# A hybrid decoder trunk on eight cores: the program rewritten with even token groups, the norm factor applied to results, and one mLSTM chain between the dense units

## What is computed

```python
# x: (8, 2048, 2048); 16 meta tokens are put ahead of each sequence
for l in range(2):
    proj = rmsnorm(h, norm_mix_w[l]) @ w_in[l]              # 2048 -> 6152
    q, k, v, og, ig, fg, u, gb, gc = jnp.split(proj, split_points, axis=-1)
    hm = mlstm_group(q, k, v, ig + b_i, fg + b_f)           # 4 heads, qk 128, v 256, chunkwise
    hm = jax.nn.sigmoid(og) * rmsnorm_per_head(hm, mlstm_norm_w[l])
    hc = gb * causal_conv3(gc * u, conv_w[l])
    h = h + jnp.concatenate([hm, hc], axis=-1) @ w_out[l]
    hf = rmsnorm(h, norm_ffn_w[l])
    h = h + (silu(hf @ w_gate[l]) * (hf @ w_up[l])) @ w_down[l]   # width 5632
return rmsnorm(h, norm_final_w)[:, 16:]
```

## Time and profile before

| | us |
|---|---|
| median of 3 runs (lowest to highest) | 6702.95 (6699.74 to 7196.77) |
| span of the profiled execution, slowest core | 6697.5 |
| TensorE matmul busy in it | 5962.8 (89%) |
| VectorE busy | 1665.9 (25%) |
| ScalarE busy | 878.2 (13%) |
| GpSimd busy | 460.8 (7%) |

### The profile page before, as it was taken

One profiled execution on the slowest core, in us unless ns is written; L12 is line 12 of the kernel. 1 busy time (PEld: TensorE's weight loads), 2 busy tenths in 40 slices (PEclk: granted clock), 3 DMA queues, 4 the chain that ended last, 5 costly groups with the idle time before them and its releaser, 6 DMA issues.

```text
span 6697.5 us, 83763 instructions; the slowest of 8 cores (6676.9 to 6697.5 us)
## 1 busy us (share of the span) xinstructions
PE 5962.8 (89%) x33182; PEld 2840.1 (42%) x33822; DVE 1665.9 (25%) x3868; ACT 878.2 (13%) x1988; POOL 460.8 (7%) x416
## 2 busy tenths in 40 slices
PE   5885999999788599999977968999998987999997
PEld 3442444444344244444443433444443433344444
DVE  2333211111333321111133432111113532211113
ACT  2212100000121210000022121000002221100002
POOL 0110000000011000000000100000000100000000
PEclk7997999999899799999988988999998998999998
DMA  4662556655365245655553654665564763655653
GB/s 83 56 61 32 60 70 73 76 70 72 49 60 57 35 59 71 73 76 70 71 125 53 67 57 51 69 79 77 71 76 54 73 62 46 69 71 74 82 77 81
DMA packets 814720, 450.64 MB, mean 67 GB/s; under 512 B 277488, under 2 KB 810096, under 8 KB 810224
## 3 DMA queue, kind: packets, MB, share of 16 engines
q0 software_dynamic: 809408, 411.20, 52.2%
q1 hardware_dynamic: 4928, 34.03, 1.4%
HBM read 839.60 MB, written 16.78 MB: 128 GB/s over the span
## 4 chain that ended last, share of the span: by engine, by line
PE 81%; DVE 9%; issue 4%; DMA 3%; ACT 3%; DVEq 0%; ACTq 0%; POOL 0%; SPq 0%; POOLq 0%
PE bank L225 80%; DVE hb L244 2%; DMA wb<-w_up 1%; PE bank L228 1%; DVE scr L244 1%; DMA mx<-x 1%; ACT scr L238 1%; DVE hmn L248 1%; DVE cstate L244 1%; ACT ep L238 1%; DMA out<-mx 0%; DVE mx L244 0%; DVE mx L241 0%; DVE tmpm L248 0%; DVE hT L244 0%
## 5 line engine op out<-in xcount | busy, mean ns | idle before, releaser
L225 PE MATMUL bank<-hb,wb 128*128 128x512 bf16 (+1 forms) x20056 | 3691.0, 339 | 119.5 <-DVE hb L244 40.9
L225 PEld LDWEIGHTS bank<-hb,wb 128*128 128x128 bf16 x20480 | 1702.7, 97 | 2078.0 <-issue 196.7
L225 PE MATMUL bank<-mx,wb 128*128 128x512 bf16 (+1 forms) x9414 | 1721.6, 337 | 18.5 <-DVE mx L241 4.9
L225 PEld LDWEIGHTS bank<-mx,wb 128*128 128x128 bf16 x9600 | 794.3, 97 | 927.1 <-issue 36.1
L241 DVE TENSOR_TENSOR mx<-bank,scr 128x512 bf16<-128x512 f32 x520 | 306.1, 589 | 2258.5 <-PE bank L225 2069.9
L238 ACT ACTIVATE scr<-bank 128x512 f32<-128x512 f32 (+3 forms) x640 | 329.3, 515 | 3559.0 <-PE bank L225 3472.1
L241 DVE TENSOR_TENSOR hT<-bank,hT 128x512 f32<-128x512 f32 (+1 forms) x800 | 425.6, 582 | 1341.5 <-PE bank L225 1277.1
L228 PE MATMUL bank<-ident_bf,hmn 128*128 128x128 bf16 (+1 forms) x272 | 41.5, 241 | 311.3 <-DVE lfrep L248 207.0
L262 POOL DMA_DIRECT2D wb<-w_in x152 | 173.9, 1154 | 1621.0 <-PE bank L225 952.3
L262 POOL DMA_DIRECT2D wb<-w_gate x88 | 100.6, 1143 | 2260.7 <-PE bank L225 2260.7
L238 ACT ACTIVATE scr<-hT 128x1040 bf16<-128x1040 f32 (+1 forms) x160 | 167.2, 1060 | 660.5 <-DVE hT L241 622.0
(11 more groups left out here) (81 smaller groups left out, 1666.5 us busy)
## 6 DMA issues: line engine op xcount, KB each, us to landing
wb<-w_gate POOLq DMA_DIRECT2D x88, 1024.0 KB, 14.1
wb<-w_up POOLq DMA_DIRECT2D x88, 1024.0 KB, 18.4
wb<-w_down POOLq DMA_DIRECT2D x48, 1536.0 KB, 12.2
wb<-w_in POOLq DMA_DIRECT2D x128, 512.0 KB, 12.2
wb<-w_out POOLq DMA_DIRECT2D x16, 2048.0 KB, 17.1
mx<-x SPq DMA_DIRECT2D x16, 1024.0 KB, 7.8
wb<-w_in POOLq DMA_DIRECT2D x8, 2048.0 KB, 17.7
wb<-w_in POOLq DMA_DIRECT2D x16, 1024.0 KB, 18.7
```

What stands on the lines that cost most here:

```text
L225: P.op("tensor", lambda e: e.matmul(out, lhsT=lhsT, rhs=rhs, start=start, stop=stop), reads, writes)
```

## The change

The same work on the same data flow, in a new program:

- Token groups. First half 348, 346 and 346 columns, the meta tokens first in the sequence; second half 512 and 512. In output projection and feed-forward of layer 1 of the first half the meta tokens are left out (512 and 512).
- A unit is one feature tile and one group: 16 matmuls into one bank (`unit`), then its evacuation.
- Norm. hb holds h times the norm's weight, not yet divided by the root mean square; the factor per token (rrow for rows, rcol for columns) is multiplied onto the results as they leave PSUM. Square sums: ScalarE squares each residual group, VectorE adds to acc, and one f32 matmul with ones per group ends them.
- Weights lie in memory as they are used, slots of 256 columns, 8 KB written per partition; four buffers, each fetched again once its slot is used up.
- One mLSTM chain over all four heads and their chunks (34 or 38 steps). It advances by a credit that each dense unit adds to (`tick`); the units of other heads' q, k, V, output gates and all conv pairs lie between its steps. Order of the slots: `PLANS`.
- In the chain: the forget sum is broadcast by the transpose itself, the mask is added in one VectorE operation, and the normaliser's squares, logarithm (with the max term as bias), exponential and scaling run on ScalarE.
- x tiles are loaded four ahead; V and q, k of heads 0 and 1 run between them, and in the second half also between the stores of the first.
- Feed-forward blocks of 15, 15 and 14 hidden tiles.
- Between operations of one engine, a write now also waits for earlier reads of the same buffer.

```diff
-FF_BLOCKS = [(0, 12), (12, 12), (24, 12), (36, 8)]
+FF_BLOCKS = [(0, 15), (15, 15), (30, 14)]
+GROUPS = [[(0, 348), (348, 346), (694, 346)], [(0, 512), (512, 512)]]
...
-                if rd.eng == eng and rd.dma_key is None and dma_key is None:
-                    continue
...
+        def tick(weight=1.0):
+            run_later()
+            if pend["steps"] is not None:
+                pend["credit"] = min(pend["credit"] + pend["rate"] * weight, 3.0)
+                while pend["credit"] >= 1.0 and step_ready():
+                    pend["credit"] -= 1.0
+                    run_step()
...
+        def unit(wap, bw, off, src, bsrc, order, g):
+            t0, tn = cur["groups"][g]
+            b = next_bank()
+            for i, k in enumerate(order):
+                mm(banks[b][:, 0:tn], wap(k, off, 128), src[:, k, t0:t0 + tn], i == 0, i == len(order) - 1,
+                   [bw] + on(bsrc[k], g), [b_bank[b]])
+            return b
...
+        def residual(f, g, b, wcol, final):
...
+            tt(h, banks[b][:, 0:tn], h, ALU.add, [b_bank[b]], on(b_hT[f], g))
...
+                act(sq, h, AF.Square, on(b_hT[f], g), [b_scr[si]])
+                tt(a, a, sq, ALU.add, [b_scr[si]], on(b_acc, g))
...
+                act(hb[:, f, t0:t0 + tn], h, AF.Copy, [b_cols] + on(b_hT[f], g), on(b_hb[f], g), scale=w)
...
+                    tt(a[:, 2:2 + tn], banks[b][:, 0:tn], r2, ALU.mult, [b_bank[b]] + on(b_acc, g), [bA])
+                    tick()
+                    b = unit(ws[c_s][0], ws[c_s][1], c_o, hb, b_hb, ALLK, g)
+                    tt(a[:, 2:2 + tn], banks[b][:, 0:tn], a[:, 2:2 + tn], ALU.mult, [b_bank[b]], [bA])
+                    tick()
+                    b = unit(ws[b_s][0], ws[b_s][1], b_o, hb, b_hb, ALLK, g)
+                    ts(cb, a[:, 2:2 + tn], wc[2], None, ALU.mult, None, [bA, b_cols], [bC])
+                    stt(cb, a[:, 1:1 + tn], wc[1], cb, ALU.mult, ALU.add, [bA, b_cols], [bC])
+                    stt(cb, a[:, 0:tn], wc[0], cb, ALU.mult, ALU.add, [bA, b_cols], [bC])
...
+                    tt(cb, cb, r1, ALU.mult, on(b_r, g), [bC])
+                    tt(mx[:, 8 + c, t0:t0 + tn], banks[b][:, 0:tn], cb, ALU.mult, [b_bank[b], bC], on(b_mx[8 + c], g))
...
+                    act(hmn[0:n, :], num_r[0:n, 0:DV], AF.Square, [bN], [b_hmn, b_ep], accum_out=ep[0:n, 0:1])
...
+                    act(ep[0:n, 4:5], ep[0:n, 0:1], AF.Ln, [b_ep], [b_ep], scale=1.0 / DV, bias=ep[0:n, 2:3])
                     act(ep[0:n, 5:6], ep[0:n, 4:5], AF.Exp, [b_ep], [b_ep], scale=-0.5)
...
+                        tt(s, banks[b][:, 0:tn], r1, ALU.mult, [b_bank[b]] + on(b_r, g), [bS])
+                        act(s, s, AF.Silu, [bS], [bS])
...
+                        tt(s, banks[b][:, 0:tn], s, ALU.mult, [b_bank[b]], [bS])
+                        tt(mx[:, j, t0:t0 + tn], s, r1, ALU.mult, [bS] + on(b_r, g), on(b_mx[j], g))
```

More of the change, by code:

```diff
@@ L17 @@
 DFF = 5632
-DIN = 6152
 NX = 1024
@@ L255, in cp @@
             else:
[L256 to L290, removed]
+                P.op("vector", lambda e: e.tensor_copy(out, in_), reads, writes)
@@ L298, in next_bank @@
             return b
[L300 to L312, removed]
@@ L456, in gates_phase @@
[L456 to L467 removed]
+        pend = {"later": [], "steps": None, "credit": 0.0, "rate": 0.0}
@@ new lines, in after, with run_later, step_ready @@
+        def after(n, fn):
+            pend["later"].append([n, fn])
+        def run_later(every=False):
+            due = []
+            for item in pend["later"]:
+                item[0] -= 1
+                if item[0] <= 0 or every:
+                    due.append(item)
+            pend["later"] = [i for i in pend["later"] if i not in due]
+            for item in due:
+                item[1]()
+        at = {"og": -1, "qk": -1, "v": -1, "A": -1, "B": -1, "s": 0}
+        def step_ready():
+            nch, s = len(cur["chunks"]), at["s"]
+            if pend["steps"] is None:
+                return False
+            t0, n = cur["chunks"][(s - 2) % nch]
+            ok_c = s < 2 or at["og"] >= len(cur["groups"]) * ((s - 2) // nch) + over(t0, n)[-1]
+            ok_b = not 1 <= s <= NH * nch or at["v"] >= (s - 1) // nch
+            ok_a = s >= NH * nch or at["qk"] >= s // nch
+            return ok_a and ok_b and ok_c
@@ new lines, in build_nc, with segs, on, over @@
+        cur = {"hf": 0, "groups": GROUPS[0], "chunks": CHUNKS[0]}
+        def segs(t0, n):
+            return [i for i in range(len(SEGS) - 1) if t0 < SEGS[i + 1] and SEGS[i] < t0 + n]
+        def on(bufs, g):
+            return [bufs[i] for i in segs(*cur["groups"][g])]
+        def over(t0, n):
+            return [g for g, (a, m) in enumerate(cur["groups"]) if t0 < a + m and a < t0 + n]
+        def unit(wap, bw, off, src, bsrc, order, g):
[5 more added lines that the diff above has]
+            return b
@@ L695, in build_nc @@
+        for i in range(8):
+            so, bso = stage(i % 4)
+            store_tile(1, GROUPS[1], i, so, bso, f"se{i % 4}")
         b_fin = [Buf("fin_act"), Buf("fin_dve")]
@@ L697, in build_nc @@
         memset(ep[0:1, 7:8], 0.0, [b_fin[1]])
-        every = [b for b in b_wb + b_bank + [b_wg]]
-        P.op("sync", lambda e: None, b_fin + every, stage_bufs(0) + stage_bufs(1))
+        ends = [b for j in range(4) for b in stage(j)[1]]
+        P.op("sync", lambda e: None, b_fin + b_wb + b_bank, ends)
         sems = {}
```

955 lines of the change are left out of this document (561 added, 394 removed), and 4 rows, old and new, of the table PLANS.

## The result

The new kernel takes 0.858 of the time of the kernel before (95% interval 0.854 to 0.861): 5746 and 5748 us where before had 6700 and 6703.

A forecast was written before the change was run, and what follows sets the result against it. TensorE bounds the feed-forward stages and waits elsewhere. Dense 5,432 us, start 105, change of half 105, end 50 and stalls 90 make 5,782 us of span, 5,788 us of time, rounded to 5,790; range 5,700 to 6,060.

The forecast's parts named there:

- the last one of the sum: Whole kernel: 5,782 us of span become 5,788 us of time, adding the 5.5 us between profiled span and median before.
- rival 3: Whole kernel: a program without holes could be granted a lower clock, at ratio 1.074 giving 6,215 us; chance 0.04.
- The price of a matmul: TensorE: a matmul of 346 to 348 columns takes 146.5 ns, three take 439.5 ns, from the sizes 128, 257 and 512.
- the bound of +186 us: First-half matmuls: upper bound if each of 10,944 short matmuls paid what the 16-column one pays beyond its columns.
- The gain by stage: Cross-check: heads phases give back about 214, 171, 169, 113 us, feed-forward 61, 75, 24, 28, projections 68, end 7.
- The dense sum: TensorE's stages without loaders and end: 2,739 us in the first half plus 2,693 in the second, 5,432 us.
- Loaders and end: Start 105 us (85 to 135), change of half 105 us (88 to 130), end of the program 50 us.
- Stalls: TensorE's remaining waits: 15 us in each heads phase, 30 us for norms and gate chains, 90 us together.
- The chain: mLSTM chain in the heads phases: steps 6 to 11 us apart; stall nil if 5.23 us plus queueing fits in 7.
- VectorE: Conv stage, first half: 21.9 us of VectorE per channel against 23.1 us of TensorE, 94% filled.
- Rival 1: Conv stage: VectorE becomes the bound, 5 us more per channel over 32 channels, 160 us, giving 5,950 us; chance 0.14.
- Weights and table loads: Weight slots land in 2.8 to 8.9 us against 14.1 of matmul, hidden; ScalarE table loads go from 49 to about 100.

The follow-up runs named there:

- e1: The new kernel with the first half's token groups set back to 512, 512 and 16 columns: 5858 us, +114 against 5744 us.
- e2: The new kernel with the credit per dense unit set to 0, so that chain steps are issued back to back: 6342 us, +597 against 5744 us.
- e7: The new kernel with four extra VectorE passes over each conv group that leave its values as they are: 5776 us, +32 against 5744 us.
- e11: The new kernel with eight extra VectorE passes over each conv group that leave its values as they are: 5958 us, +214 against 5744 us.
- e4: The new kernel with weights held in memory in rows of 256 columns and written 512 bytes at a time: 5752 us, +8 against 5744 us.

## Why the prediction was right, and where it was wrong

The forecast of 5,788 us stands 0.7% above the 5746 and 5748 us of the comparison, and the ratio was expected at 0.864 and is 0.858. The recorded time missed all the same: the median over all runs is 6186 us, outside 5,700 to 6,060. The step that failed is the last one of the sum, from 5,782 us of span to 5,788 us of time, together with rival 3, the clock, and its chance of 0.04. That step takes every execution to be granted the clock of the dense windows. In four of six executions it was not so: they took 6030 to 6583 us. I had set rival 3 against dense windows of one execution at 1.00, and the earlier trace rows can't rule out other executions; I had its price (1.074) from the spread of three runs in the table, and gave an event that had shown in one of three runs 1 in 25.

Rival 3's price was right, 6,215 us against 6186. Its condition was not: it made a program without holes the cause. The kernel before, with all its holes, took 7197 to 7383 us in four of its six runs; the clocks of these were not kept, but runs of it beside the experiments that took 7393 and 7399 us have a mean clock of 0.84 on one die and 0.94 on the other. For both kernels the median of all six stands 7.7% above the fastest. That is also why the ratio came out and the time did not.

The windows of cores 2 and 5 over the same stretch of the profiled execution of the new kernel, and one of core 0:

```profile
30.00:1650.00 1620.00, 1614.45 (x9370) 1015.04 (x9371) 517.80 (x1189) 277.15 (x680) 48.39 (x92) 0.81 0.36 64
```
```profile
30.00:1650.00 1620.00, 1610.72 (x11377) 1103.58 (x11378) 636.75 (x1506) 395.64 (x976) 58.08 (x110) 1.00 0.44 76
```
```profile
4550.00:5950.00 1400.00, 1390.51 (x5276) 584.25 (x5383) 385.96 (x629) 167.17 (x315) 43.79 (x83) 0.81 0.40 61
```

0.81 is the 13/16 of the Trainium skill ("TensorE: Matmul & The Clock Gate", Part 1), and with it 0.82 of the matmuls are done in the same time. The Trainium skill has it come for a whole die once three of its cores run dense matmuls, and hold while the load lasts. Here cores 2 and 3 have it from about 40 to about 1700 us of their spans and then 1.00 with TensorE as busy as before; cores 0 and 1 of the same die have 1.00 at first and 0.81 only from about 4500 us to the end (each core's times count from its own start); cores 4 to 7 never have it, and in two of the six executions no core has (mean clock 0.994 to 0.997). What starts and ends it no run of mine tells. It stays open.

By its own steps:

- *The price of a matmul.* 146.5 ns foreseen, 211.6 us / 1440 = 146.9 measured. The ladder from 128, 257 and 512 columns was right, and nothing of the bound of +186 us came. e1 confirms the 26 ns of the short one.
- *The gain by stage.* The heads phases with what lies ahead of them give back 216, 179, 171 and 122 us, where 214, 171, 169 and 113 were foreseen; feed-forward 54, 78, 18 and 21 against 61, 75, 24 and 28; the projections 68 as foreseen; the end 26 against 7.
- *The dense sum.* Feed-forward of layer 0 928 us foreseen, 937.2 measured, the other three 913 to 918 where 910 was foreseen; projections 112.5 and 110, measured 114.0 and 111 to 114; heads of layer 1 with 15 us of stalls 384 and 369, measured 375.8 and 359.7.
- *Loaders and end.* Start with its heads phase and 15 us of stalls 429 foreseen, 426.5 measured; change of half with its heads phase and 15 of stalls 419, measured 417.2 (2880 to 3297.2). The end was over-priced: 50 us against 31.5.
- *Stalls.* This term was mis-sized: 90 us foreseen, and outside the loaders and the end TensorE is idle for only some 12. The sum came out near because the stages run longer than their priced matmuls (feed-forward by 25 us, loaders with their heads phases by 26, heads of layer 1 by 12, projections by 8), less 18 at the end: 53 us where 90 stood. That these errors largely cancel is luck.
- *The chain.* Hidden as forecast. I had read 5.23 us of latency from the kernel before; the bare period of a full step was 6.68 us there and is 5.36 now (e2), which two units of 2.34 us and a step's matmuls just cover.
- *VectorE.* 94% foreseen in the conv stage, 67% busy measured, 78% with the pauses that the forecast counted in. The single durations were right (0.52 us for 346 columns). Too high were the pauses (about 8 us in the window of 18 conv groups, where 7 of 0.11 us were booked for each group) and the steps (0.31 a unit in the layer that I show, not 0.34), and some neighbouring operations overlap. Rival 1 is real where VectorE is full (e7, e11).
- *Weights and table loads.* Landing in 9.9 us against 14.1 of matmul; 79 table loads where I had said about 100. Both hidden.

Undone one at a time, the parts give: weaving 597 us, norm on the results 136, groups with their segments 84 to 114, loaders 25, normaliser 14, rows of the weights 8: 864 to 894 us of the 953 between the spans. They need not add, and the kernel before had a weaving of its own, so the 597 is not what it gained from this part. The same-engine waits, the four weight buffers and the feed-forward blocks were not tried alone.

## What to carry to other kernels

A latency chain beside dense work needs a spacing, not an amount: find its bare period (here 5.36 us), count the dense work between two of its steps, and give credit by time, not by unit. An engine is full when it no longer waits for its inputs, which was here at 82% busy; read that, and not the share. Where a factor per token can go onto the results, the pass over the operands ahead of a stage goes from the path. And a fetch that is held back by reading a live buffer makes that buffer's next writer wait for the transfer.

## What the runs showed of the hardware that was not expected

- On core 5 of the new kernel the first groups of 16 f32 transposes took 3.65, 3.65 and 3.47 us, later ones 1.91 us, while the clock of each of these windows is given as 1.00. They run at half the later rate in spite of the row; on core 1 the row for 31 to 36 us says 0.50. In the first 40 us the row of one core is not to be relied on.
- A matmul of 16 columns costs 26 ns whether it stands beside one of 512 or in a row of 16 with a weight tile each (457.0 and 456.9 ns for the three).
- The same 411 MB take 61.2% of the DMA engines in 809,504 packets and 42.8% in 57,888 (e4 and the new kernel, core 5).
- Two cores of a die can be granted 0.81 while the other two are at 1.00 for the same part of the program (core 2 and core 0 of the profiled execution, above).
